# First feed-forward group: all of its up half on features without the norm, and the rewriting moved into its down half

## What is computed

```
def rmsnorm_2(x, g):                       # rmsnorm_3 is the same
    y = xf * lax.rsqrt(jnp.mean(xf * xf, axis=-1, keepdims=True) + EPS)
    return (y * g.astype(jnp.float32)).astype(x.dtype)

# second block (D_FF = 2816)
hn = rmsnorm_2(h, norm_ffn[l])
g, up = jnp.split(hn @ w_ffn_in[l], 2, axis=-1)
h = h + (jax.nn.silu(g) * up) @ w_ffn_out[l]

# third block (D_FF_3 = 4096)
m = rmsnorm_3(h, norm_mlp_g[l]) @ w_mlp_up[l].astype(h.dtype)
h = h + jnp.square(jax.nn.relu(m)) @ w_mlp_down[l].astype(h.dtype)
```

## Time and profile before

| what | value |
|---|---|
| median of three runs | 3790.49 us (3788.84 to 3791.66) |
| profiled execution | 3788.43 us |
| its span, first to last instruction | 3786.6 us |
| PE busy | 3385.2 us, 89% |
| PEld / DVE / ACT / POOL busy | 72% / 35% / 19% / 33% |
| mean granted TensorE clock | 0.948 |
| f2, first group | up half to 1930.4 us, down half to 1974.3 us |
| f3, first group | up half to 3099.1 us, down half to 3143.0 us |

### The profile page before, as it was taken

The page is one execution under the profiler, slowest core; times in us unless marked ns, Lnnn a source line. Parts: engine busy times, 40 slices in busy tenths (PEclk is TensorE's granted clock), DMA queues, the critical chain, the costliest instruction groups (busy, mean ns, idle before and its releaser), DMA issues.

```text
span 3786.6 us, 37633 instructions
## 1 busy us (share of the span) xinstructions
PE 3385.2 (89%) x15562; PEld 2712.5 (72%) x15562; DVE 1325.3 (35%) x1659; ACT 734.1 (19%) x1080; POOL 1231.0 (33%) x1052
## 2 busy tenths in 40 slices
PE   5957976899959899999999999994888989999997
PEld 4546855678848578787788888883875768888886
DVE  4154065123150630413611111126898562222223
ACT  2220054121020630101300000003333320000101
POOL 3201301335313023334433433431442334334331
PEclk9978998999979899999999999996989989999998
DMA  3100100102121001012111111111002001111111
GB/s 116 45 17 28 45 1 23 56 34 89 55 84 56 1 25 66 34 56 87 36 56 45 44 54 46 44 55 63 34 27 74 34 34 45 55 44 44 55 44 44
DMA packets 31635, 179.48 MB, mean 47 GB/s; under 512 B 3744, under 2 KB 4768, under 8 KB 14624
## 3 DMA queue, kind: packets, MB, share of 16 engines
q1 hardware_dynamic: 18864, 137.37, 10.6%
q10 hardware_dynamic: 12656, 40.42, 2.9%
HBM read 163.10 MB, written 14.68 MB: 47 GB/s over the span
## 4 chain that ended last, share of the span: by engine, by line
PE 79%; DVE 14%; ACT 3%; issue 2%; POOL 1%; DMA 0%; DVEq 0%; ACTq 0%; POOLq 0%
PE ps L428 45%; PE ps L461 16%; PE ps L487 5%; PE ps L1755 2%; DVE c_out L2181 2%; PE ps L1854 1%; PE ps L1392 1%; PE ps L744 1%; PE ps L1408 1%; DVE n_sq L355 1%; ACT p L911 1%; PE ps L300 1%; DVE xlo L361 1%; DVE n_acc L287 1%; PE ps L308 1%
## 5 line engine op out<-in xcount | busy, mean ns | idle before, releaser
L527 POOL TENSOR_TENSOR whi<-raw,par 128x512 fp32r<-128x512 f32 x131 | 150.0, 1145 | 2449.6 <-PE ps L428 1759.8
L531 POOL TENSOR_TENSOR wlo<-raw,whi 128x512 fp32r<-128x512 f32 x524 | 796.8, 1521 | 41.7
L428 PE MATMUL ps<-xhi,whi 128*128 128x512 f32 x2304 | 723.9, 396 | 47.3 <-DVE xlo L361 14.9
L428 PE MATMUL ps<-xlo,whi 128*128 128x512 f32 x2304 | 716.3, 392 | 0.0
L428 PE MATMUL ps<-xhi,wlo 128*128 128x512 f32 x2304 | 715.6, 392 | 0.0
L428 PEld LDWEIGHTS ps<-xhi,whi 128*128 128x128 f32 x2304 | 434.9, 190 | 152.9 <-issue 23.4
L428 PEld LDWEIGHTS ps<-xlo,whi 128*128 128x128 f32 x2304 | 437.6, 190 | 92.7
L428 PEld LDWEIGHTS ps<-xhi,wlo 128*128 128x128 f32 x2304 | 436.5, 189 | 92.2
L529 POOL CAST whi<-raw 128x512 fp32r<-128x512 f32 x393 | 305.7, 778 | 0.0
L1284 DVE TENSOR_TENSOR h<-h,ps 128x1024 f32<-128x1024 f32 x112 | 132.2, 1217 | 414.1 <-PE ps L461 414.1
L461 PE MATMUL ps<-hidden_lo,whi 128*128 128x512 f32 x864 | 269.1, 393 | 0.0
(11 more groups left out here) (435 smaller groups left out, 4013.9 us busy)
## 6 DMA issues: line engine op xcount, KB each, us to landing
raw<-stream SPq DMA_DIRECT2D x131, 1024.0 KB, 4.8
h_scr<-h ACTq DMA_DIRECT2D x2, 4096.0 KB, 12.1
x_in<-xT ACTq DMA_DIRECT2D x4, 1024.0 KB, 14.4
x_again<-xT ACTq DMA_DIRECT2D x4, 1024.0 KB, 8.0
h<-h_scr ACTq DMA_DIRECT2D x1, 4096.0 KB, 12.9
outT<-h ACTq DMA_DIRECT2D x8, 512.0 KB, 3.0
bias<-bias ACTq DMA_DIRECT2D x1, 2560.0 KB, 18.5
o_scr<-o_staged ACTq DMA_DIRECT2D x2, 1024.0 KB, 4.8
```

The source lines that it names most:

```text
L428: mm = nc.tensor.matmul(ps[:, c0 + c:c0 + c + width], w, x(k, a, width), start=(n == 0 and m == 0), stop=(n == len(ks) - 1 and m == 2))
L527: nc.gpsimd.tensor_tensor(WHI[:, r, t], RAW[:, r, t], one, ALU.mult).then_inc(hi_done, 1)
L531: ins = nc.gpsimd.tensor_tensor(WLO[:, r, t], RAW[:, r, t], WHI[:, r, t].bitcast(F32), ALU.subtract)
```

## The change

The up half of the first group, in f2 and in f3, takes raw features for all of its output blocks. `kept` is waited for ahead of tile (2, 0), since the norm's sums lie in the PSUM quad that is used next. norm_columns goes ahead of tile (0, 7) in both. Each of the 4 hidden blocks is multiplied by `kept` on its way out of PSUM: two multiplications by DVE with Silu in place on ACT in f2, `relu_raw` on DVE in f3. The rewriting of the 8 feature blocks moves into DVE's part of the down half: features 0 to 3 ahead of the first additions, feature 4 ahead of the third, 5 to 7 ahead of the fifth, the last low part ahead of the sixth. ACT starts its high copies when the last up quad is ready. PE and ACT wait for all rewritten low parts ahead of the second group. The results of norm_again go to a new tile `again`, which lies where ff_act lies. PE's signals norm_used go.

```diff
         def norm_hi_again(act, N, last_raw):
+            act.wait_ge(quad_ready, last_raw + 1)
             for b in range(KB):
                 act.wait_ge(*of(N, "x", b + 1))
-                if b < KB - 1:
-                    act.wait_ge(*of(N, "used", b + 1))
-                else:
-                    act.wait_ge(quad_ready, last_raw + 1)
-                nc.scalar.activation(N["hi"](b), N["sq"][:, b % 2, :], ACT.Copy).then_inc(S("norm_hi"), 1)
+                nc.scalar.activation(N["hi"](b), N["again"][:, b % 2, :], ACT.Copy).then_inc(S("norm_hi"), 1)
...
                     if ready and o == 0:
                         pe.wait_ge(*ready(n))
-                    if raw and o == raw[1]:
-                        pe.wait_ge(*of(raw[0], "lo", KB + n + 1))
...
-            before = N and {(0, 5 if k == "f2" else 6): lambda: norm_columns(pe, N), (1, 2): lambda: norm_spread(pe, N)}
+            before = N and {(0, 7): lambda: norm_columns(pe, N), (1, 2): lambda: norm_spread(pe, N),
+                            (2, 0): lambda: pe.wait_ge(*of(N, "kept", 1))}
             feature_tiles(pe, up_where, outs, range(KB), xhi, xlo, sloop=sl, qloop=ql, o_per_quad=outs // n,
-                          before=before, raw=N and (N, RAW_OUTS))
+                          before=before, ready=N and (lambda m: of(N, "lo", m + 1)))
...
+            if N:
+                norm_hi_again(act, N, up_quad + n - 1)
...
+        AGAIN = {0: (0, 4), 2: (4, 5), 4: (5, KB)}
...
-                if k == "f2" and first and j == 0:
+                if k == "f2" and first:
                     dve.wait_ge(quad_ready, q + 1)
-                    nc.vector.tensor_tensor(FA[:, 0, :], half(q, 0), first["kept"][:, :], ALU.mult).then_inc(free(q), 1)
-                    nc.vector.tensor_tensor(FT[:, 0, :], half(q, 1), first["kept"][:, :], ALU.mult).then_inc(free(q), 1)
-                    dve.wait_ge(*L("ff_raw", 1))
+                    nc.vector.tensor_tensor(FA[:, j % 2, :], half(q, 0), first["kept"][:, :], ALU.mult).then_inc(free(q), 1)
+                    nc.vector.tensor_tensor(FT[:, j % 2, :], half(q, 1), first["kept"][:, :], ALU.mult).then_inc(free(q), 1)
+                    dve.wait_ge(*L("ff_raw", j + 1))
...
+                    if first:
+                        relu_raw(dve, first, j, q)
...
             for b in range(KB):
                 q = down_quad + b // 2
+
+                if first and b in AGAIN:
+                    norm_again(dve, first, *AGAIN[b])
+                if first and b == 5:
+                    norm_low_again(dve, first, KB - 1)
                 dve.wait_ge(quad_ready, up(q + 1, ql))
...
             pe_group(pe, k, 4, *at_group(0), 0, None, N)
+            pe.wait_ge(*of(N, "lo", 2 * KB))
...
             act_group(act, k, 4, at_group(0)[0][1], 0, None, N)
+            act.wait_ge(*of(N, "lo", 2 * KB))
...
             dve.wait_ge(*of(NRMP, "kept", 1))
-            up_q = WH["up_3_0"][1]
-            relu_raw(dve, NRMP, 0, up_q)
-            norm_again(dve, NRMP, 0, 5)
-            relu_raw(dve, NRMP, 1, up_q + 1)
-            norm_again(dve, NRMP, 5, KB)
-            norm_low_again(dve, NRMP, KB - 1)
-            dve.wait_ge(*of(NRMP, "lo", 2 * KB))
             dve_groups(dve, "f3", H3, NRMP, NRME)
```

More of the change, by code:

```diff
@@ L246, in build @@
         raw_loaded = [S("raw_loaded0"), S("raw_loaded1")]
-        norm_counts = dict(sq=0, add=0, sum=0, root=0, recip=0, diag=0, inv=0, x=0, hi=0, lo=0, used=0, kept=0)
+        norm_counts = dict(sq=0, add=0, sum=0, root=0, recip=0, diag=0, inv=0, x=0, hi=0, lo=0, kept=0)
         def norm_set(name, src, n, gain, scr, before, nb=KB, hi=None, lo=None, out=None, bank=0, spread_at=None):
@@ L263, in norm_set @@
                 N["kept"] = at(f"{name}_spread", spread_at, [P, n])
-                norm_counts["used"] += nb - 1
+                N["again"] = at(f"{name}_again", A + 32768, [P, 2, n])
                 norm_counts["kept"] += 1
@@ L367, in norm_again @@
                     dve.wait_ge(*of(N, "lo", KB + b - 1))
-                nc.vector.scalar_tensor_tensor(N["sq"][:, b % 2, :], N["src"](b), N["gain"](b), N["kept"][:, :],
+                nc.vector.scalar_tensor_tensor(N["again"][:, b % 2, :], N["src"](b), N["gain"](b), N["kept"][:, :],
                                                ALU.mult, ALU.mult).then_inc(S("norm_x"), 1)
@@ L374, in norm_low_again @@
             dve.wait_ge(*of(N, "hi", KB + b + 1))
-            nc.vector.tensor_tensor(N["lo"](b), N["sq"][:, b % 2, :], N["hi"](b).bitcast(F32), ALU.subtract)\
+            nc.vector.tensor_tensor(N["lo"](b), N["again"][:, b % 2, :], N["hi"](b).bitcast(F32), ALU.subtract)\
                 .then_inc(S("norm_lo"), 1)
         def norm_hi_again(act, N, last_raw):
+            act.wait_ge(quad_ready, last_raw + 1)
             for b in range(KB):
                 act.wait_ge(*of(N, "x", b + 1))
-                if b < KB - 1:
-                    act.wait_ge(*of(N, "used", b + 1))
-                else:
-                    act.wait_ge(quad_ready, last_raw + 1)
-                nc.scalar.activation(N["hi"](b), N["sq"][:, b % 2, :], ACT.Copy).then_inc(S("norm_hi"), 1)
+                nc.scalar.activation(N["hi"](b), N["again"][:, b % 2, :], ACT.Copy).then_inc(S("norm_hi"), 1)
         def norm_hi(act, N):
@@ L401, in feature_tiles @@
         def feature_tiles(pe, where, outs, ks, xhi, xlo, chunks=((0, HALF, 0), (HALF, HALF, BANK)), ready=None,
-                          qloop=None, sloop=None, o_per_quad=2, before=None, raw=None, last=None):
-            if raw:
-                ready = lambda n: of(raw[0], "lo", n + 1)
+                          qloop=None, sloop=None, o_per_quad=2, before=None, last=None):
             slot, quad = where
@@ L432, in feature_tiles @@
                             first = False
-                    if raw and o == raw[1] - 1 and n < KB - 1:
-                        mm.then_inc(S("norm_used"), 1)
                     if last and o == outs - 1 and n < len(ks) - 1:
@@ L1212, in build @@
         hlo = lambda k, a, w: HL[:, k, a:a + w]
-        RAW_OUTS = 2
         def pe_group(pe, k, n, up_where, down_where, blocks_before, loop, N=None):
@@ L1229, in made @@
         def made(eng, k, j, up_quad, blocks_before, loop, N):
-            if k == "f2" and N and j == 0:
-                eng.wait_ge(*L("ff_x", 1))
+            if k == "f2" and N:
+                eng.wait_ge(*L("ff_x", j + 1))
             elif k == "f2":
@@ L1241, in act_group @@
                 q = up_quad + j
-                if N and k == "f2" and j == 0:
+                if N and k == "f2":
                     act.wait_ge(free(q), freed(q, 0))
-                    nc.scalar.activation(FA[:, 0, :], FA[:, 0, :], ACT.Silu).then_inc(S("ff_raw"), 1)
-                elif not N or k == "f2" or j >= RAW_OUTS:
+                    nc.scalar.activation(FA[:, j % 2, :], FA[:, j % 2, :], ACT.Silu).then_inc(S("ff_raw"), 1)
+                elif not N:
                     act.wait_ge(quad_ready, up(q + 1, ql))
@@ L1262, in dve_group @@
                     dve.wait_ge(S(k + "_lo"), up(blocks_before + j - 1, bl))
-                if k == "f2" and first and j == 0:
+                if k == "f2" and first:
                     dve.wait_ge(quad_ready, q + 1)
-                    nc.vector.tensor_tensor(FA[:, 0, :], half(q, 0), first["kept"][:, :], ALU.mult).then_inc(free(q), 1)
-                    nc.vector.tensor_tensor(FT[:, 0, :], half(q, 1), first["kept"][:, :], ALU.mult).then_inc(free(q), 1)
-                    dve.wait_ge(*L("ff_raw", 1))
+                    nc.vector.tensor_tensor(FA[:, j % 2, :], half(q, 0), first["kept"][:, :], ALU.mult).then_inc(free(q), 1)
+                    nc.vector.tensor_tensor(FT[:, j % 2, :], half(q, 1), first["kept"][:, :], ALU.mult).then_inc(free(q), 1)
+                    dve.wait_ge(*L("ff_raw", j + 1))
                     dve.wait_ge(free(q), freed(q, 1))
-                    nc.vector.tensor_tensor(FT[:, 0, :], FA[:, 0, :], FT[:, 0, :], ALU.mult).then_inc(S("ff_x"), 1)
+                    nc.vector.tensor_tensor(FT[:, j % 2, :], FA[:, j % 2, :], FT[:, j % 2, :], ALU.mult).then_inc(S("ff_x"), 1)
                 elif k == "f2":
@@ L1552, in act_block2 @@
             norm_keep(act, NRMG)
-            norm_hi_again(act, NRMG, WH["up_2_0"][1])
-            act.wait_ge(*of(NRMG, "lo", 2 * KB))
             act_groups(act, "f2", NRMG)
@@ L1671, in dve_block2 @@
             dve.wait_ge(*of(NRMG, "kept", 1))
-            norm_again(dve, NRMG, 0, KB)
-            norm_low_again(dve, NRMG, KB - 1)
-            dve.wait_ge(*of(NRMG, "lo", 2 * KB))
             dve_groups(dve, "f2", H2, NRMG, NRMO)
@@ L2106, in act_block3 @@
             norm_keep(act, NRMP)
-            norm_hi_again(act, NRMP, WH["up_3_0"][1] + RAW_OUTS - 1)
-            act.wait_ge(*of(NRMP, "lo", 2 * KB))
             act_groups(act, "f3", NRMP)
```

## The result

| | before | after |
|---|---|---|
| median | 3789.62 us (5 runs) | 3770.10 us (5 runs, 3766.74 to 3772.37) |
| ratio | | 0.9943, 95% interval 0.9930 to 0.9955 |
| profiled execution / its span | 3788.43 / 3786.6 us | 3772.37 / 3770.5 us |
| mean granted clock | 0.948 | 0.946 |

The forecast was 3771 us. Since two executions of the same code can differ by several us somewhere else, I read the two profiles by stretches of the first groups. "f2 up" runs from the start of tile (0,0), counted back from norm_columns at 1.363 us a tile, to the first matmul of the down half. "f3 up" runs from the end of tile (0,5), where the wait begins, to the first matmul of the down half.

The account below looks back on a forecast made before the run. TensorE (busy 89% of the span) was taken as the bound, except while DVE rewrites features with the norm. 9.0 + 12.0 + 1.0 - 2.4 + 0 = 19.6 us gained, median about 3771 us, range 3766 to 3778.

Parts of the forecast that it names:

- The waits at output block 2: Up halves: TensorE no longer waits for features rewritten with the norm; 9.0 us gained in f2, 12.0 in f3.
- The columns in f2: norm_columns moved behind tile (0,6) in f2 no longer meets its wait; 1.0 us gained, bounds 0 and 2.6.
- The columns in f3: norm_columns behind tile (0,6) in f3: start 1.1 us later, one more half-speed tile at 1.3; 2.4 us lost.
- The down half: 16 DVE and 8 ACT instructions moved there in each layer meet TensorE's deadlines; price 0.
- The chain of the last output: DVE and ACT work on f2's last up output, reaching into the down half; done 8.3 us in.
- The rewriting of the first four features: Features 0 to 3 in f2's down half: 5.3 us against POOL plus 5.0 mostly without, done at 18.6.
- The pairs beside POOL: One L368 and one L375 on DVE while POOL splits weights: 1.5 and 2.3, 3.76 us a pair.
- Rival 2: Down half: quad 0's deadline missed, 1.6 us wait in f2, 0.5 in f3; 3773, or 3777 if others miss; chance 0.11.
- the slack: f2's down half: features 0 to 3 done 0.8 us ahead of the first additions' 19.4 us deadline.
- Rival 3: Wait moves to group 1's start, moved DVE instructions waiting out GpSimd ones; 25 us a layer, about 3820; chance 0.02.
- the deadline of quad 0: Down half: TensorE needs PSUM quad 0 freed at 16 tiles, 22.0 us from its start.
- The total: Sum of the gains and losses over both layers: 19.6 us gained, median 3770.9 us.

Follow-up runs that it names:

- the f2-only kernel: New scheme in f2 only, f3 as in the kernel before, against the changed kernel: median 3778.76 us, ratio 0.997 to before.
- The first experiment: Changed kernel with norm_columns back ahead of tile (0,5) in f2 and (0,6) in f3: median 3768.0 us.
- the two kernels with the old place: Changed kernel with f3's norm_columns ahead of (0,6); f2's ahead of (0,5) in one, (0,7) in the other: medians 3768.0 and 3770.9 us.
- the kernel with five features first: Changed kernel with feature 4 rewritten ahead of the down half's first addition instead of the third: median 3773.61 us.
- the kernel with features 6 and 7 first: Changed kernel with f3's raw features 6 and 7 written ahead of the norm's last squares and additions, norm_columns at (1,2), norm_spread at (1,5): 3760.15 us.

## Why the prediction was right

- **The waits at output block 2.** 9.0 and 12.0 forecast, 9.2 and 12.0 measured; the f2-only kernel brings back f3's part with its low clock, as the second half of that term said.
- **The columns in f2.** The one term that was clearly off: 1.0 taken, 2.7 measured, just past its bound of 2.6. The step took the wait alone and left the half-clock tiles behind it as a bound. The first experiment shows that the two go together: with the columns at their old place the 1.0 us of idle time came back, and 1.7 us of clock with it. Whether the wait alone does it, or only ahead of the columns, isn't shown; four longer waits ahead of full tiles in f2 left the clock at 1.00.
- **The columns in f3.** 2.4 lost forecast; 2.2 in the profile, 2.1 by the two kernels with the old place. The order of the terms was right: a later start, and one more tile at 1.2 GHz.
- **The down half.** Price 0 forecast and measured. The chain of the last output was done at 7.0 instead of 8.3 us, since beside POOL the product and L1279 (here L1274) took 1.4 and 1.7 us instead of 2.4 and 2.3. The rewriting of the first four features then took 11.2 us instead of 10.3, since more of it stood against POOL; that 18.2 came so close to 18.6 is two misses of about 1 us that cancel. The pairs beside POOL took 3.79 us (3.76 forecast), in f2 divided otherwise: L368 2.2 and L375 1.6 instead of 1.5 and 2.3. Rival 2 needed a chain longer by more than the slack; the kernel with five features first shows that one pair does it.
- **Rival 3** asked for 2.4 us per instruction; the worst pair gave 1.9. Its size was never near, but the risk of the moved work was: put in the wrong place, the same sixteen instructions cost 22.6 us in both layers together, by the deadline of quad 0 and not by dearer instructions.
- **The total.** 21.7 us by the stretches, 19.6 forecast; of the difference 1.7 are the columns in f2. The 19.5 between the medians agrees with the forecast to 0.1 us by luck: the sum missed by 2.1 us, and medians of the kernel before alone lie 1.6 us apart.

## What to carry to other kernels

Where a scale can be applied to the results, apply it to the results until the engine that rescales the operands has a stretch to itself; then price the moved work against each deadline of the stretch that takes it up, since one pair too many ahead of the first deadline costs a wait and everything ahead of it can cost the gain. Before a producer's chain is moved, ask which of its outputs the waiting engine needs first: here two features were worth 7 us and the norm's sums could wait. And where TensorE has just stood idle, try full tiles first and the one-column sums later: here it gave 3.2 us.

## What the runs showed of the hardware

A short wait can cost more than itself by the clock, and not by its length alone: 1.0 us of idle time ahead of the sixteen one-column matmuls brought 1.7 us more, in both kernels that have it. Four waits of 1.7 to 2.1 us between full tiles in f2 left the granted clock at 1.00, four of 0.8 to 2.3 us in f3 brought it to 0.69, and a single one of 2.3 us, in the kernel with features 6 and 7 first, brought some 3 us at the low clock. What sets these apart wasn't tried.

POOL loses as well: with DVE at work on two SBUF inputs for much of the down half, its busy time went from 16.9 to 25.6 us in 44 us for the same two splits. At about 13 us each they fit into their slots of 22 us, and PE didn't wait.
